# Order changes across a two-block transformer kernel: first mixer, grouped-query and later mixers, borders between stages

## The reference, cut to what matters

```python
x = first_block(x)        # layer 0: rmsnorm, latent attention + dilated attention, projection, swiglu
                          # layer 1: rmsnorm, grouped-query attention (16 heads, 4 kv heads), swiglu
return second_block(x)    # twice: half swiglu, a mixer of three branches with gates, half swiglu
...
z = rmsnorm(x, mix_norm_ab[i]) @ w_in_ab[i]
o_a = mla_mixer(z[..., :IN_A], ...); o_b = dilated_mixer(z[..., IN_A:], slopes)
x = x + concatenate([o_a, o_b]) @ w_out_ab[i]
...
q = rmsnorm(q, q_gain); k = rmsnorm(k, k_gain)              # grouped-query layer
o = blocked_attention(axial(q), axial(k), v, scale); x = x + o @ w_o
...
g_a, g_b, g_c = split(sigmoid(h @ w_merge_gate + b_merge_gate), 3)
mix = g_a * (y_a @ w0) + g_b * (y_b @ w1) + g_c * (y_c @ w2); x = x + mix @ w_o
```

## Time and profile before

| | before |
|---|---|
| median of 3 runs | 1963.28 us (1960.85 to 1963.84) |
| the profiled execution, own time | 1960.66 us |
| its span, first to last instruction | 1958.9 us |
| PE, DVE, ACT, POOL busy | 98%, 69%, 43%, 6% |
| mean granted TensorE clock | 0.996 |
| read from memory | 174 GB/s over the span |

### The profile page before, as it was taken

How to read it: one execution, slowest core, us unless ns; L and a number is a source line. 1 busy time by engine, 2 the same in 40 slices (tenths; PEclk the granted TensorE clock), 3 DMA queues, 4 the chain that set the end, 5 groups by cost and what they waited for, 6 DMA issues and landing times.

```text
span 1958.9 us, 30216 instructions
## 1 busy us (share of the span) xinstructions
PE 1910.8 (98%) x11674; PEld 1687.0 (86%) x11674; DVE 1347.5 (69%) x1702; ACT 841.3 (43%) x1051; POOL 119.0 (6%) x146
## 2 busy tenths in 40 slices
PE   7999999989999999999999999999999999999998
PEld 7988888877888888888899888888888899998887
DVE  5676777766777777774666677777776566677776
ACT  4555334454334433443354443343344335444333
POOL 1001200420000100000200100000000020010000
PEclk9999999999999999999999999999999999999999
DMA  7423555424555555534334455566554443354552
GB/s 294 173 87 138 197 193 188 156 77 172 209 191 193 233 193 193 189 144 157 145 130 149 163 215 193 193 224 224 186 185 176 150 143 139 112 211 183 193 191 109
DMA packets 47595, 342.27 MB, mean 175 GB/s; under 512 B 5344, under 2 KB 5376, under 8 KB 7440
## 3 DMA queue, kind: packets, MB, share of 16 engines
q1 hardware_dynamic: 43200, 313.02, 44.1%
q0 software_dynamic: 4304, 27.95, 3.7%
HBM read 339.89 MB, written 1.05 MB: 174 GB/s over the span
## 4 chain that ended last, share of the span: by engine, by line
PE 91%; DVE 5%; ACT 2%; issue 1%; POOL 0%; DMA 0%; ACTq 0%; DVEq 0%; POOLq 0%
PE bank L996 23%; PE bank L812 17%; PE bank L814 16%; PE bank L813 16%; PE bank L995 10%; PE bank L1097 2%; PE bank L871 2%; PE bank L1073 2%; DVE wlo L1817 1%; PE bank L998 1%; ACT whi L1413 1%; PE bank L1273 1%; DVE x L1899 0%; ACT y L1451 0%; DVE y L1863 0%
## 5 line engine op out<-in xcount | busy, mean ns | idle before, releaser
L1817 DVE TENSOR_TENSOR wlo<-raw,whi 128x2048 fp32r<-128x2048 f32 x296 | 680.0, 2300 | 252.2 <-ACT whi L1413 251.1
L1413 ACT ACTIVATE whi<-raw 128x2048 fp32r<-128x2048 f32 x296 | 564.9, 1909 | 238.5 <-PE bank L814 235.0
L996 PE MATMUL bank<-ysp,whi 128*128 128x512 f32 x1920 | 666.0, 396 | 0.0
L995 PE MATMUL bank<-ysp,wlo 128*128 128x256 f32 x1680 | 468.4, 279 | 0.0
L996 PEld LDWEIGHTS bank<-ysp,whi 128*128 128x128 f32 x1920 | 347.6, 188 | 67.0
L995 PEld LDWEIGHTS bank<-ysp,wlo 128*128 128x128 f32 x1680 | 316.7, 189 | 10.7
L1495 ACT ACTIVATE sg<-sg 128x256 f32<-128x256 f32 x120 | 50.2, 418 | 468.9 <-DVE sg L1946 468.9
L812 PE MATMUL bank<-ysp,wlo 128*128 128x256 f32 x720 | 208.5, 290 | 5.2 <-DVE nv L2294 2.2
L812 PE MATMUL bank<-whi,hl 128*128 128x512 f32 x528 | 206.1, 390 | 0.0
L814 PE MATMUL bank<-whi,hh 128*128 128x512 f32 x528 | 205.4, 389 | 0.0
L813 PE MATMUL bank<-wlo,hh 128*128 128x512 f32 x528 | 205.4, 389 | 0.0
(11 more groups left out here) (317 smaller groups left out, 2421.4 us busy)
## 6 DMA issues: line engine op xcount, KB each, us to landing
raw<-stream SPq DMA_DIRECT2D x296, 1024.0 KB, 4.8
sr<-side POOLq DMA_DIRECT2D x10, 1024.0 KB, 7.4
gbc<-gains POOLq DMA_DIRECT2D x11, 512.0 KB, 3.9
cw<-small POOLq DMA_DIRECT2D x2, 2048.0 KB, 10.3
dbias<-dilb POOLq DMA_DIRECT2D x1, 2304.0 KB, 10.2
lng<-rows POOLq DMA_DIRECT2D x2, 1024.0 KB, 5.2
tab<-second POOLq DMA_DIRECT2D x1, 1724.0 KB, 17.1
x<-xin SPq DMA_DIRECT2D x2, 512.0 KB, 6.6
```

The source lines that it names most:

```text
L995: pe.matmul(o[:, 0, :], lo[:, k, cols], yh[:, k, :], start=False, stop=False, skip_group_check=True)
L996: last = pe.matmul(o, hi[:, k, cols], ysp[:, :, k, :], start=k == 0, stop=k == 7)
L1413: act.activation(whi[s], raw[s], ACT.Copy).then_inc(hi_made, 1)
L1817: dve.tensor_tensor(wlo[s], raw[s], whi[s].bitcast(F32), ALU.subtract).then_inc(lo_made, 1)
```

## The change

The first tile is split in four quarters, and `opening_step` consumes it quarter by quarter; 18 matmuls of ones come before it. In the first mixer two query steps and two key-value steps go behind the transposes of the softmax (`behind`), and the heads are transposed in another order, so that four batches, not six, stand before the first latent scores. In the grouped-query part one projection goes behind the second group's scores, a head batch goes into a step, `late_heads` moves, seven copies go from DVE to ACT, and DVE splits a weight tile in quarters during turns 4 to 7. In the later mixers two copies go ahead of a tile split on DVE, the first gate steps alternate banks, and one copy goes from DVE to ACT. At four borders ACT makes the second high quarter before its last sum of squares and DVE makes the first low quarter before its last addition. The last feed-forward layer no longer turns its result, and the output is stored by three DMAs. The core of the diff (declarations, helper arguments and the head order repeated on ACT and DVE are left out):

```diff
--- before.py
+++ after.py
@@ -111,7 +111,7 @@
-PLAN1.batches("mqk", "AD" * 4)
+PLAN1.batches("mqk", "ADADAAAD")
@@ -120,7 +120,7 @@
-PLAN1.batches("gqa", "AD" * 8)
+PLAN1.batches("gqa", "ADADADAAAAAAAAAD")
@@ -132,7 +132,7 @@
-PLAN2.batches("cmp", "AD")
+PLAN2.batches("cmp", "AA")
@@ -146,6 +146,7 @@
+GATE_BANKS = (1, 0, 1) + (0,) * 9
...
@@ -636,7 +641,7 @@
-        late_heads = {0: 2, 2: 3, 4: 4}
+        late_heads = {1: 2, 2: 3, 4: 4}
@@ -657,13 +662,17 @@
-            sp.wait_ge(out_ready, 1)
-            sp.dma_start(out, y).then_inc(out_done, 16)
-            sp.wait_ge(out_done, 16)
+            sp.wait_ge(y_ready, 46)
+            sp.dma_start(out[:, 0, :], y[:, 0, :]).then_inc(out_done, 16)
+            for q in range(2):
+                sp.wait_ge(y_ready, 47 + q)
+                sp.dma_start(out[:, 1, 512 * q:512 * q + 512], y[:, 1, 512 * q:512 * q + 512]).then_inc(out_done, 16)
+            sp.wait_ge(out_done, 48)
...
+            pool.memset(ones, 1.0).then_inc(ones_set, 1)
@@ -956,11 +965,11 @@
-            def dense(B, stage, i, kind, kc=8, w=256, c0=0, n=256, act=(yh, yl), per_tile=1, bank=None, alone=False, late=None, skipped=0):
+            def dense(B, stage, i, kind, kc=8, w=256, c0=0, n=256, act=(yh, yl), per_tile=1, bank=None, alone=False, late=None, skipped=0, others=False):
...
-                bank_free(B, step, i == 0 or alone)
+                bank_free(B, step, (i == 0 or alone) and not others)
...
@@ -1118,20 +1129,35 @@
+            pe.wait_ge(ones_set, 1)
+            for _ in range(18):
+                pe.matmul(pb[4][:, 0:P], ones, ones, start=True, stop=True)
...
-            keep_warm(12, 0)
-            copied(B, 2)
+            keep_warm(12, 5)
...
-            def second_half():
-                turn(B, "n0", 0, 1, 0)
-                turn(B, "n0", 0, 1, 1)
-                copied(B, 4)
-            for i in range(9):
-                dense(B, "z", i, "T" if i < 3 else "F", n=160 if i == 2 else 256, late=((1, 0), second_half) if i == 0 else None)
+            def opening_step():
+                hi, lo = rows3(whi[0], 8, 256), rows3(wlo[0], 8, 256)
+                for m in range(M):
+                    t = slice(m * P, m * P + P)
+                    if m:
+                        turn(B, "n0", 0, 1, 0)
+                        turn(B, "n0", 0, 1, 1)
+                    for k in range(8):
+                        if m == 0 and k % 2 == 0:
+                            pe.wait_ge(first_hi, k // 2 + 1)
+                            pe.wait_ge(first_lo, k // 2 + 1)
+                        if k % 4 == 0:
+                            copied(B, 2 * m + k // 4 + 1)
+                        last = three(pb[0][:, 256 * m:256 * m + 256], (yh[:, k, t], yl[:, k, t]), (hi[:, k, :], lo[:, k, :]), k == 0, k == 7)
+                last.then_inc(step_done, 1)
+            opening_step()
+            for i in range(1, 9):
+                dense(B, "z", i, "T" if i < 3 else "F", n=160 if i == 2 else 256)
@@ -1145,8 +1171,8 @@
-                src = (mq, kasm)[j // 4]
-                batch(B, tb_mqk + j, [src[:, m, 2 * (j % 4) + k, :] for k in range(2) for m in range(M)], DK1)
+                src = (mq, kasm)[j // 2 % 2]
+                batch(B, tb_mqk + j, [src[:, m, 4 * (j // 4) + 2 * (j % 2) + k, :] for k in range(2) for m in range(M)], DK1)
@@ -1157,35 +1183,41 @@
-                    queries(1)
...
-                    copied(B, tb_cq + 3)
-                    keys_values(0)
...
-                    keys_values(2)
...
-                    for j in range(4):
+                    head_T(0)
+                    head_T(1)
+                    pe.wait_ge(drain_act, B.drained(B.plan.step["ukv"] + 4, "A"))
+                    pe.wait_ge(kr_spread, 1)
+                    head_T(2)
+                    head_T(3)
+            def behind(i):
+                if i == 2:
+                    queries(1)
+                if i == 4:
+                    copied(B, tb_cq + 3)
+                    keys_values(0)
+                if i == 5:
+                    keys_values(2)
+            needs = {g: lambda g=g: pe.wait_ge(drain_act, B.drained(B.plan.step["z"] + 7 + g, "A")) for g in range(DG)}
+            attention(B, "dil", dil_groups(), AG_DIL, beside, needs, behind)
+            def between_heads(i):
+                if i == 0:
+                    for j in range(4, 8):
...
-            needs = {g: lambda g=g: pe.wait_ge(drain_act, B.drained(B.plan.step["z"] + 7 + g, "A")) for g in range(DG)}
-            attention(B, "dil", dil_groups(), AG_DIL, beside, needs)
-            pe.wait_ge(drain_act, B.drained(B.plan.step["ukv"] + 4, "A"))
-            pe.wait_ge(kr_spread, 1)
-            head_T(4)
-            head_T(5)
-            def between_heads(i):
-                if i == 0:
-                    head_T(6)
-                    head_T(7)
@@ -1195,7 +1227,7 @@
-            attention(B, "mla", mla_groups(), AG_MLA, between_heads, {0: lambda: copied(B, tb_mqk + 6), 2: lambda: copied(B, tb_mqk + 8)})
+            attention(B, "mla", mla_groups(), AG_MLA, between_heads, {0: lambda: copied(B, tb_mqk + 4), 2: lambda: copied(B, tb_mqk + 8)})
@@ -1232,7 +1264,7 @@
-                if i == 0:
+                if i == 1:
@@ -1247,9 +1279,8 @@
-                dense(B, "gqkv", i, "T", skipped=1)
-            for u in range(2):
-                batch(B, tb_gqk + u, head_blocks(u))
+                dense(B, "gqkv", i, "T", skipped=1, late=((1, 0), lambda: batch(B, tb_gqk, head_blocks(0))) if i == 4 else None)
+            batch(B, tb_gqk + 1, head_blocks(1))
@@ -1355,20 +1386,20 @@
-                dense(B, "gates", 0, "F", bank=0)
...
+                    dense(B, "gates", m, "F", bank=GATE_BANKS[m], others=True)
...
-                dense(B, "gates", 1, "F", bank=0, alone=True)
...
+                pe.wait_ge(bd_ready, l + 1)
...
-                    dense(B, "gates", 2 + i, "F", bank=0, alone=True)
+                    dense(B, "gates", 2 + i, "F", bank=GATE_BANKS[2 + i], alone=True, others=i < 2)
@@ -1392,7 +1423,7 @@
-                ffn(B, "fb", 3 + 2 * l, "n6", 7 + 3 * l, (B.following(), "n4", 8 + 3 * l))
+                ffn(B, "fb", 3 + 2 * l, "n6", 7 + 3 * l, (B.following(), "n4", 8 + 3 * l) if l < LAYERS - 1 else None)
@@ -1462,12 +1493,15 @@
-            def ending(B, n, norm_stage, then=None):
+            def ending(B, n, norm_stage, then=None, late=False):
...
+                if late:
+                    hi_norm(then or B, norm_stage, 0, 1)
...
-                hi_norm(then or B, norm_stage, 0, 1)
+                if not late:
+                    hi_norm(then or B, norm_stage, 0, 1)
@@ -1556,7 +1590,12 @@
-            split(B, 0)
+            act.wait_ge(landed[0], 16)
+            for q in range(4):
+                c = slice(512 * q, 512 * q + 512)
+                act.activation(whi[0][:, c], raw[0][:, c], ACT.Copy).then_inc(first_hi, 1)
+            act.wait_ge(first_hi, 4)
+            act.sem_inc(hi_made, 1)
...
@@ -1644,7 +1682,8 @@
-                    head_T(6)
+                    for j in (4, 5, 6):
+                        head_T(j)
@@ -1655,7 +1694,7 @@
-            ending(B, 2, "n2")
+            ending(B, 2, "n2", late=True)
@@ -1702,12 +1741,12 @@
-            attention(B, "gqa", gqa, AG_GQA, None, lambda i: queries(5) if i == 0 else None, between)
+            attention(B, "gqa", gqa, AG_GQA, None, lambda i: queries(5) if i == 1 else None, between)
...
+            ahead(B, "gwo", 1)
...
-            for t in (1, 2):
-                ahead(B, "gwo", t)
+            ahead(B, "gwo", 2)
@@ -1719,7 +1758,7 @@
-                ending(B, 6 + 3 * l, "n5")
+                ending(B, 6 + 3 * l, "n5", late=True)
@@ -1756,15 +1795,17 @@
-                        ins = act.activation(gates[:, j, :], bank2(0)[:, c, :], ACT.Tanh, bias=hmb[:, j:j + 1], scale=0.5)
+                        ins = act.activation(gates[:, j, :], bank2(GATE_BANKS[i])[:, c, :], ACT.Tanh, bias=hmb[:, j:j + 1], scale=0.5)
...
-                act.wait_ge(tb_done, B.tb0 + tb + 1)
-                act.activation(PT2[0][0:120, 0, 0, :], pb[B.bank(tb)][0:120, 0:P], ACT.Copy).then_inc(tb_act, 1)
-                gate_drain(1)
+                for m in range(M):
+                    if m:
+                        gate_drain(1)
+                    act.wait_ge(tb_done, B.tb0 + tb + m + 1)
+                    act.activation(PT2[0][0:120, m, 0, :], pb[B.bank(tb + m)][0:120, 0:P], ACT.Copy).then_inc(tb_act, 1)
@@ -1787,7 +1828,10 @@
-                ending(B, 8 + 3 * l, "n4", B.following())
+                if l < LAYERS - 1:
+                    ending(B, 8 + 3 * l, "n4", B.following(), late=True)
+                else:
+                    sumsq(8 + 3 * l)
@@ -1815,6 +1859,15 @@
+            def split_quarter(B, tile, q):
+                s, c = B.slot(tile), slice(512 * q, 512 * q + 512)
+                if q == 0:
+                    dve.wait_ge(hi_made, B.tile_no(tile) + 1)
```

(81 more changed lines are left out.)

6 lines of the change are left out of this document (removed).

## The result

| | before | after |
|---|---|---|
| time, median | 1962.36 us (1960.85 to 1963.84, 4 runs) | 1929.54 us (1929.48 to 1929.58, 4 runs) |
| the profiled execution | 1960.66 us, span 1958.9 | 1929.48 us, span 1927.7 |
| TensorE's mean granted clock | 0.996 | 0.999 |

The ratio is 0.9833, with a 95% interval of 0.9816 to 0.9850: 32.8 us less between the medians, 31.2 less between the profiled executions. The forecast was 1930.5 in a range of 1924.5 to 1939.0.

What follows compares the result with a forecast made beforehand. PE is busy 98%, so time returns only at its waits, its low clock and the two ends. Terms summed to 31.05 us off 1960.66, 1929.6; the forecast was 1930.5, its own range 1926 to 1934, the full range 1924.5 to 1939.

Steps and rivals of the forecast that it cites:

- The opening: Start of the kernel: splitting in quarters and ones that raise the clock bring PE's second half forward, -3.4 us.
- The first mixer: First mixer: steps between softmax transposes hide ACT's drains (-2.4) and the `mkT` wait of 0.8 goes; -2.85 us in all.
- The borders: Four stage borders: DVE's low part ahead of its last addition starts 0.6 us earlier each time; -2.4 us.
- The grouped-query attention: Grouped-query stretch: waits and low clock of 9.5 go, delays of 0.4 and 0.9 come; -8.2 us.
- The later mixers: Two later mixers: `bdrow` 2.3, `nv` 2.2, `gates` 2.2, `p` 2.2 and low clock 3.3 go; -12.2 us.
- The end: End of the kernel: two transpose batches go (0.4 and 0.1) and the split store gains 1.5; -2.0 us.
- The low clock comes back: Rival: light work also lowers PE's clock, in two or three stretches, +3.1 + 3.3, at most 1937 us; chance 0.17.
- ACT becomes late in the grouped-query part: Rival: copies, exponentials and high parts queue on ACT; up to 5.6 back plus low clock, 1936 to 1940; chance 0.10.
- The ones don't raise the clock: Rival, opening: PE pauses between the ones and y, so the clock stays low; +2.9, about 1933 us; chance 0.05.
- Slower: Rival: unfilled attention turns hold the clock low through whole mixers, about 2030 us; chance 0.03.
- no change: Rival: each wait is replaced by one on the next engine, 1960 us; chance 0.02.
- the signs: Profile checks: among them no `bdrow` wait beyond 0.3; a `pt` wait over 1 us in all would show a rival.

Runs made afterwards that it cites:

- the filler in the kernel before: Kernel before, plus eight unread matmuls in the 1.8 us pause ahead of the first clock fall: 1958.86 us against 1961.02.
- whole split: Changed kernel, with DVE splitting the second `gwo` tile whole behind turn 6, not in quarters in turns 4 to 7: 1932.81 us against 1929.45.
- one gate bank: Changed kernel, with all gate steps of the later mixers in bank 0 and the other drains waited for: 1940.52 us against 1929.45.
- four more moves: Changed kernel, plus both batches in the last projection step, earlier keys copy, earlier `gwo` product, gate drain behind the `pt` copies: 1932.65 us against 1929.45.
- both grouped-query batches behind the step: Changed kernel, with the first head batch taken out of the last projection step, both behind it: 1928.92 us against 1929.45, the fastest version.
- `bdrow` behind the split: Changed kernel, with the two short DVE copies in both later mixers put back behind the tile split of 2.29: 1932.19 us against 1929.45.
- the shared copies: Changed kernel, with the grouped-query softmax transposes' copies alternating between ACT and DVE again: 1929.37 us against 1929.45.
- the old borders: Changed kernel, with DVE's addition ahead of the low part and ACT's sum of squares ahead of the second high part, four borders: 1932.14 us against 1929.45.
- nothing behind the softmax: Changed kernel, with the first mixer's query and key-value steps back to back again, not behind the softmax's transposes: 1932.14 us against 1929.45.
- the one store: Changed kernel, with the whole output stored by one 1 MB DMA as before: 1931.16 us against 1929.45.

## Why the prediction was right, and where it was off

**The sum, 1929.6 against 1929.48 measured in the profiled execution**, is nearer than its terms are. By its own steps:

- *The opening, 3.4.* 3.2. Each of its times came within 0.25: first matmul on weights 12.18 (12.3), second half 17.79 (17.6), transposes 1.23 (1.0), filler 2.84 (2.6). That the ones raise the clock is shown by the run without them.
- *The first mixer, 2.85.* 3.2 by position. By waits, `mq` and `mkv` gave 2.4 as predicted, and taking those steps back cost 2.7. Among the head batches I was right in the size and not in the place: I had DVE's wait staying, 0.8 going and 0.35 coming. Before, PE waited 0.25 and 0.9 among the batches and 0.8 behind them; after, 0.45, 0.7 and 0.25, all for ACT's copies. DVE's, of which this is the line in the waits before, is gone:

```profile
PE bank L871 <- DVE mqT L1838: 0.9, 1, 0.9
```

- *The borders, 2.4.* 2.6: 0.65 at each of four; taking it back cost 2.7. The cover for the later addition held.
- *The grouped-query attention, 8.2.* 9.1. The low clock was 3.1, as predicted, and the filler in the kernel before gives nearly the same: from the product behind the fall to the end of the stretch, 430.83 to 463.43 became 430.99 to 460.71, 2.9 less. The pauses gave 5.2 against 9.5 - 3.1 - 0.4 - 0.9 = 5.1, but two of their terms were wrong and cancel, which was luck. The copies on ACT cost 0, not 0.9, and are four, not the seven that the text counted. And of the wait on `p`, counted as gone, 1.0 is still there, one turn on. The 0.9 between 8.2 and 9.1 is busy time of PE that the sum did not have. The inserted batch cost its 0.4 (`gkT` 0.8 to 1.2), and undoing it gave 0.5 back.
- *The later mixers, 12.2.* 10.6. `nv`, `gates`, `p` and the clock gave 2.2, 2.2, 2.2 and 3.2, as predicted. Two terms failed. `bdrow` gave 1.8, not 2.3: 0.4 a layer stays, since DVE's two copies (893.03 and 893.12) can begin only when PE's product that feeds them has ended (893.00), and PE goes on at 893.39: they are on the path, and no order of DVE's takes them off it. And ACT's copy of `pt` behind a gate drain, which the text had at "0 to 0.3 a layer" and the sum at nothing, costs 0.5 a layer. The timeline shows it plainly: ACT's gate drain of 0.84 from 950.48 stands ahead of its 0.28 copy, and PE is ready at 951.05 and goes on at 951.54.
- *The end, 2.0.* 2.4; the store alone is 1.7 by its own run (1.5 predicted).

**The range's reason to go up did not come.** The forecast stood 0.9 above the sum, because the median of the runs shown stood 2.6 above the profiled execution and "the runs after may stand so too". They don't: they lie within 0.1 us. The spread belongs to the kernel before. That its falls come in some executions at other places, or not at all, is the likely reason; only one execution of each kernel was profiled.

**The rivals.** *The low clock comes back*: no. The only windows of the changed kernel under 1.00 lie behind PE's last matmul. The prediction feared that light work alone would let it fall; in the profiled runs here no stretch of light work did so without a pause near it. But three experiments made it fall again: by a pause of 1.8 (whole split), by one of 2.8 and in the next mixer one of 1.1 (one gate bank), and by one of 2.9 (four more moves).

The length of a pause alone does not decide. The prediction names two waits of 1.8 ahead of the first two falls; there is a third in the kernel before, the 1.8 on `wlo` from 450.73 to 452.52, and the clock stayed at 1.00 through it and behind it:

```profile
450.73:456.00 5.27, 3.47 (x15) 2.93 (x16) 4.45 (x3) 1.38 (x3) 0.00 (x0) 1.00 0.40 141
```

The run with both grouped-query batches behind the step paused as long between the ones and the first transposes, and these still took 1.23, as at the upper clock:

```profile
8.49 1.23 PE L880 MATMUL bank<-misc,y 128*128 128x128 f32 x8 [1.77 <-DVE y L1917]
```

The 1.1 on `nv`, on the other hand, had a fall behind it or in it at three of six places (one each in the kernel before, with the filler, and with one gate bank), while the 1.2 on `gkT` never had one. What the pauses with a fall have in common is not shown. *ACT becomes late in the grouped-query part*: no, to 0.1 us. *The ones don't raise the clock*: no, 1.7. *Slower* and *no change*: neither. Of the signs, the wait on `bdrow` (0.4, not 0.3) was missed, and that on `pt`, "over 1 us in all", stood at 1.0, on the edge.

The prediction set a rule of the Trainium skill (TensorE: Matmul & The Clock Gate, What's actually happening) against the rows: the clock falls after idleness, as seen through a window that runs free of the kernel. The runs bear out the first half in part: every fall in mid-kernel stands at a pause or within 1.5 us behind one, and with the pauses the falls went, but a pause of 1.8 can pass without one. The second half fits what they show, without being proved by it: the same instructions had their fall at one place in the first later mixer and at another in the second, and the filler exchanged the two.

**What stays open.** Why the third fall in the earlier trace rows came at a pause of only 1.1, and longer ones passed without. What the 0.9 of busy time in the grouped-query stretch was. Whether the two longer runs with `bdrow` behind the split had a fall. And a version that joins the fastest run here with the later gate drain: the trace of the four moves shows the `pt` wait gone, 0.5 a layer, so some 1 us more may be there; no run has the two alone.

## What to carry to other kernels

On a kernel whose main engine is busy 98% of the time, list its waits by place and ask of each which single instruction stood ahead of the needed one; an order change that puts the short, awaited operation first is worth at most the duration of what stood ahead of it (0.65 of 0.69 at each border, but only 0.9 of a split of 2.29 for `bdrow`, since its own input came late). Other work of PE put into a wait can hide the whole of it (0.8 for each drain). Price a pause of TensorE at its length plus, perhaps, the clock: here a fall behind a pause of 1.1 to 2.9 cost another 1.6 to 3.4, though not every such pause was followed by one. So even a filler that leaves the wait as it is can pay (2.2), and a real product moved into the pause can pay twice; but look where that product is taken from, since its old place may have needed it more. A kernel whose runs spread by 2 or 3 us when others spread by 0.1 may be showing such a pause.

## What the runs showed of the hardware that was not expected

- The spread of the runs goes with the clock, with two exceptions. The changed kernel, the shared copies, the old borders, nothing behind the softmax, the grouped-query batches behind the step and the one store, whose profiles have no low window before the end, spread by 0.1 to 0.3 us. The exceptions are the kernel without ones, 0.8, and `bdrow` behind the split, 1.7, whose profiles have no low window either. The kernels with a low window spread by 1.4 (four more moves) to 3.2 (whole split), and the kernel before by 3.1.
- A pause of 1.8 need not drop the clock (450.73 in the kernel before), and the times of a kernel with such pauses can fall into two groups: 1957.7 to 1958.3 and 1959.4 to 1959.7 for the kernel before with filler.
- The granted clock in the windows reads 1.00 in the first microseconds, where most of PE's matmuls of ones still go at half pace. The 36 records take 7.1 us; 12 of them fall into 2 us at first and 10 into 1 us at the end, and the column is the same for both.

```profile
1.01 7.10 PE L1134 MATMUL bank<-ones 128*128 128x128 f32 x36 [1.01 <-POOL ones L675]
```

```profile
2.00:4.00 2.00, 2.00 (x12) 2.00 (x11) 0.00 (x0) 0.04 (x1) 0.13 (x1) 1.00 0.83 223
7.00:8.00 1.00, 1.00 (x10) 0.92 (x9) 0.39 (x1) 0.00 (x0) 0.56 (x1) 1.00 1.07 451
```

So at the start of a program the spacing of the matmuls tells the clock, and the column does not.
